# Neighbourhood attention in an encoder layer: bias tables per tile row in one transfer, split waits for queries and keys, first values on ScalarE's queue

## What is computed

```
h = rms_norm(x); proj = h @ w_in -> u, q, k, v, gates
a = fourier_mix(u) @ w_fa;  n = neighbourhood_attention(q, k, v, rpb) @ w_nb
x = x + (sig(gA) * a + sig(gB) * n) @ w_out
x = x + (silu(gate) * val) @ w_down,  [val, gate] = dwconv3(rms_norm(x) @ w_up)
return rms_norm(x)
```

## Time and profile before

| | us |
|---|---|
| median of 3 runs | 2940.61 |
| lowest and highest | 2940.39, 2942.86 |
| the profiled execution's own time | 2952.27 |
| its span, first to last instruction | 2950.5 |
| attention phase in it | about 795 to 1128 |

### The profile page before, as it was taken

One profiled execution on the slowest core, in us unless ns is written; L12 is line 12 of the kernel. 1 busy time (PEld: TensorE's weight loads), 2 busy tenths in 40 slices (PEclk: granted clock), 3 DMA queues, 4 the chain that ended last, 5 costly groups with the idle time before them and its releaser, 6 DMA issues. The chain is left out here.

```text
span 2950.5 us, 33892 instructions
## 1 busy us (share of the span) xinstructions
PE 2737.9 (93%) x12792; PEld 2274.7 (77%) x12792; DVE 1404.5 (48%) x2280; ACT 886.3 (30%) x1595; POOL 877.5 (30%) x491
## 2 busy tenths in 40 slices
PE   7999999998768896999985999997999999999997
PEld 5888888877657785777774888885888888888886
DVE  4300000006458785544336999998565554122232
ACT  3311111112345551211224444443222223343332
POOL 1010011103222224333204666664000004555553
PEclk9999999999879997999997999998999999999999
DMA  4322144426565645555535777776666665564653
GB/s 140 97 93 72 55 133 152 148 96 220 168 155 149 162 125 165 179 186 169 174 107 208 278 280 278 275 285 221 223 221 221 222 221 193 178 204 139 206 175 111
DMA packets 235537, 522.34 MB, mean 177 GB/s; under 512 B 47732, under 2 KB 73200, under 8 KB 231664
## 3 DMA queue, kind: packets, MB, share of 16 engines
q1 hardware_dynamic: 214128, 499.21, 51.3%
q10 hardware_dynamic: 21248, 20.97, 2.1%
HBM read 336.55 MB, written 185.10 MB: 177 GB/s over the span
## 5 line engine op out<-in xcount | busy, mean ns | idle before, releaser
L2205 PE MATMUL ff_psum<-ff_w,ff_hid 128*128 128x512 f32 x2112 | 479.3, 389 | 1.3 <-POOL ff_w L1798 1.3
L2205 PEld LDWEIGHTS ff_psum<-ff_w,ff_hid 128*128 128x128 f32 x2112 | 396.4, 188 | 84.1 <-POOL ff_w L1798 1.7
L1798 POOL TENSOR_TENSOR ff_w<-ff_st,ff_w 128x512 fp32r<-128x512 f32 x176 | 249.5, 1425 | 634.0 <-ACT ff_w L2041 633.6
L1798 POOL TENSOR_TENSOR ff_w<-ff_wraw,ff_w 128x512 fp32r<-128x512 f32 x154 | 269.1, 1749 | 240.9 <-ACT ff_w L2041 240.9
L422 PE MATMUL in_psum<-in_hA,in_w 128*128 128x512 f32 x1440 | 327.9, 389 | 0.0
L422 PEld LDWEIGHTS in_psum<-in_hA,in_w 128*128 128x128 f32 x1440 | 270.4, 188 | 56.0
L2166 PE MATMUL ff_psum<-ff_h,ff_w 128*128 128x512 f32 x1056 | 247.4, 393 | 27.2 <-DVE ff_h L1864 27.2
L2166 PEld LDWEIGHTS ff_psum<-ff_h,ff_w 128*128 128x128 f32 x1056 | 200.5, 190 | 70.6 <-POOL ff_w L1798 28.6
L2166 PE MATMUL ff_psum<-ff_h,ff_again 128*128 128x512 f32 x1056 | 244.7, 391 | 4.0 <-DVE ff_h L1864 4.0
L2166 PEld LDWEIGHTS ff_psum<-ff_h,ff_again 128*128 128x128 f32 x1056 | 199.3, 189 | 45.9 <-issue 4.4
L1464 PE MATMUL mo_psum<-mo_act,mo_w 128*128 128x512 f32 x768 | 191.8, 407 | 33.8 <-POOL mo_act L1315 21.0
(11 more groups left out here) (181 smaller groups left out, 4031.2 us busy)
## 6 DMA issues: line engine op xcount, KB each, us to landing
split<-ff_w SPq DMA_DIRECT2D x154, 512.0 KB, 3.6
ff_again<-split SPq DMA_DIRECT2D x154, 512.0 KB, 4.1
ff_st<-in_w_down_dram SPq DMA_DIRECT2D x176, 256.0 KB, 2.9
ff_wraw<-in_w_up_dram SPq DMA_DIRECT2D x44, 512.0 KB, 5.7
hidden<-ff_c SPq DMA_DIRECT2D x44, 512.0 KB, 3.0
ff_kraw<-hidden SPq DMA_DIRECT2D x44, 512.0 KB, 4.3
at_bias<-shifted SPq DMA_DIRECT2D x72, 256.0 KB
in_raw<-in_w_in_dram SPq DMA_DIRECT2D x32, 512.0 KB, 5.0
```

The source lines that it names most:

```text
L1798: nc.gpsimd.tensor_tensor(split_out(i, 1), parts(i), f32(split_out(i, 0)), ALU.subtract).then_inc(w_tail, 1)
L2205: last = nc.tensor.matmul(ps[:, 4 * (1 - half) + t], hid[:, a, (b * PAIRS + pair) % 2, q, t * P:(t + 1) * P], weights(i)[:, e], start=(r = ...
```

## The change

The DRAM tensor `shifted` gets the order head, query column, row, column kind, key column, and the bias and window tiles the order row kind, row, column kind, key column. So the three tables of a tile-row kind are one transfer of 768 KB, whose row for a partition is one run of 6 KB; its outermost count stays 8. In DVE's and POOL's instructions a table is now 16 rows of 32 floats, 96 floats apart. There is one bias semaphore for each row kind; SP waits, before it issues a kind's tables for head h, for that kind's tables of head h-1. `qk_in` becomes `q_in` and `k_in`: SP issues a head's queries as soon as `q_tail` of the head before is done, then waits for `k_tail` and issues the keys; ACT's first query part waits for the queries alone and its first key part for the keys. Head 0's value transfers move from SP's queue, behind three bias tables, to ACT's, ahead of its first casts.

```diff
-                sp.dma_start(shifted[j, :, c], padded[:, :, BASE_C[j] - c:BASE_C[j] - c + KC]
+                sp.dma_start(shifted[:, c, :, j], padded[:, :, BASE_C[j] - c:BASE_C[j] - c + KC]
...
-            for half in range(2):
-                for dst, src in ((qraw, qT), (kraw, kT)):
+            for dst, src, landed in ((kraw, kT, k_in), (qraw, qT, q_in)):
+                for half in range(2):
...
-                                 src[0:HEAD_DIM, :]).then_inc(qk_in, 16)
+                                 src[0:HEAD_DIM, :]).then_inc(landed, 16)
...
-        bias = m.sb("bias", [P, 2, NB, KR * KC])
-        window = m.sb("window", [P, NB, KR * KC])
+        bias = m.sb("bias", [P, 2, KINDS, KR, KINDS, KC])
+        window = m.sb("window", [P, KINDS, KR, KINDS, KC])
...
+        def load_values(engine, h):
+            run = VG * HEAD_DIM
+            for j in range(TJ):
+                rows = v[h]
+                src = bass.AP(rows.tensor, rows.offset + COL0[j] * run, [[GRID_W * run, 4], [run, KC], [1, run]])
+                engine.dma_start(vs[:, h % 2, j * VG:(j + 1) * VG].rearrange("p g d -> p (g d)"), src
+                                 ).then_inc(v_in[h % 2], 16)
...
-                for j in range(KINDS):
...
-                    rows = shifted[j, h]
-                    src = bass.AP(rows.tensor, rows.offset + (BASE_R[i] - (QR - 1)) * KC,
-                                  [[KC, QR], [REL_R * KC, QC], [1, KR * KC]])
-                    sp.dma_start(bias[:, h % 2, i * KINDS + j], src).then_inc(
-                        first_in if h == i == 0 else bias_in[h % 2], 16)
...
+                rows = shifted[h]
+                run = KINDS * KC
+                src = bass.AP(rows.tensor, rows.offset + (BASE_R[i] - (QR - 1)) * run,
+                              [[run, QR], [REL_R * run, QC], [1, KR * run]])
+                sp.dma_start(bias[:, h % 2, i].rearrange("p r j c -> p (r j c)"), src).then_inc(bias_in[i], 16)
+
+            def load_raw(h):
+                for dst, src, landed, split in ((qraw, qT, q_in, q_tail), (kraw, kT, k_in, k_tail)):
+                    sp.wait_ge(split, whole(h - 1))
+                    for half in range(2):
+                        sp.dma_start(dst[half * HEAD_DIM:(half + 1) * HEAD_DIM].rearrange("p r c -> p (r c)"),
+                                     src[h * HEAD_DIM:(h + 1) * HEAD_DIM, :]).then_inc(landed, 16)
 
             def load(h):
-                if h:
-                    sp.wait_ge(q_tail, whole(h - 1))
-                    sp.wait_ge(k_tail, whole(h - 1))
...
+                if h == 0:
+                    for i in range(KINDS):
+                        load_bias(0, i)
+                    return
+                load_raw(h)
                 if h >= 2:
                     sp.wait_ge(s_red, TILES * (h - 1))
-                if h == 0:
-                    load_bias(0, 0)
-                    load_values(0)
-                    load_bias(0, 1)
-                    load_bias(0, 2)
-                    return
                 for i in range(KINDS):
+                    sp.wait_ge(bias_in[i], 16 * h)
                     load_bias(h, i)
                 if h >= 2:
                     sp.wait_ge(o_mm, TILES * (h - 1))
-                load_values(h)
+                load_values(sp, h)
...
-                       in1=bias[:, h % 2, kind], scale=-1.0, scalar=3.0e38,
+                       in1=bias[:, h % 2, KIND[i], :, KIND[j]], scale=-1.0, scalar=3.0e38,
...
-                b = bias[:, h % 2, kind]
-                V.tensor_tensor(b, b, window[:, kind], ALU.add).then_inc(bias_ready, 1)
+                dve.wait_ge(bias_in[kind // KINDS], 16 * (h + 1))
+                b = bias[:, h % 2, KIND[i], :, KIND[j]]
+                V.tensor_tensor(b, b, window[:, KIND[i], :, KIND[j]], ALU.add).then_inc(bias_ready, 1)
...
-                if part == (0 if h else PARTS):
-                    act.wait_ge(qk_in, 64 * (h + 1))
+                if part % PARTS == 0:
+                    act.wait_ge((q_in, k_in)[part // PARTS], 32 * (h + 1))
...
+            load_values(act, 0)
             for part in (PARTS, PARTS + 1, 0, PARTS + 2, PARTS + 3, 1, 2, 3):
                 qk_head(0, part)
```

More of the change, by code:

```diff
@@ L465, in _, with fourier_phase @@
                     n += 1
-def fourier_phase(nc, step, steps, low, raw, qk_in, qT, kT, u, pos_table, chan_table, fnT_out, gate_w, b_gate, gT_out):
+def fourier_phase(nc, step, steps, low, raw, q_in, k_in, qT, kT, u, pos_table, chan_table, fnT_out, gate_w, b_gate, gT_out):
     A = SEQ // P
@@ L855, in window_mask, with attention_phase @@
     return np.concatenate([rows.reshape(P, KINDS * KR), cols.reshape(P, KINDS * KC)], axis=1)
-def attention_phase(nc, const_in, low, raw, qk_in, qT, kT, v, shifted, mask, eye, atT_out):
+def attention_phase(nc, const_in, low, raw, q_in, k_in, qT, kT, v, shifted, mask, eye, atT_out):
     KT = KR * KC // P
@@ L887, in attention_phase @@
         ps = m.banks()
-        v_in, bias_in = m.sems("v_in", 2), m.sems("bias_in", 2)
+        v_in, bias_in = m.sems("v_in", 2), m.sems("bias_in", KINDS)
         sides_in, window_done = m.sem("sides_in"), m.sem("window_done")
-        first_in = m.sem("first_in")
         qk_heads, q_tail, k_tail, bias_ready = (m.sem(x) for x in ("qk_heads", "q_tail", "k_tail", "bias_ready"))
@@ L936, in load @@
-            def load(h):
-                if h:
-                    sp.wait_ge(q_tail, whole(h - 1))
-                    sp.wait_ge(k_tail, whole(h - 1))
[L940 to L943, removed]
+                rows = shifted[h]
@@ L978, in window_kind @@
                 down = bass.AP(c.tensor, c.offset, [c.ap[0], [0, KR], [1, KC]])
-                G.tensor_tensor(window[:, i * KINDS + j].rearrange("p (r c) -> p r c", c=KC), across, down,
+                G.tensor_tensor(window[:, i, :, j], across, down,
                                 ALU.add).then_inc(window_done, 1)
@@ L1019, in reduce @@
                     dve.wait_ge(p_exp, n - 2)
-                V.tensor_tensor_reduce(out=neg[:, n % 3], in0=ps[:, SB[n % 3]],
-                                       in1=bias[:, h % 2, kind], scale=-1.0, scalar=3.0e38,
+                V.tensor_tensor_reduce(out=neg[:, n % 3].rearrange("p (r c) -> p r c", c=KC),
+                                       in0=ps[:, SB[n % 3]].rearrange("p (r c) -> p r c", c=KC),
+                                       in1=bias[:, h % 2, KIND[i], :, KIND[j]], scale=-1.0, scalar=3.0e38,
                                        op0=ALU.add, op1=ALU.min, accum_out=negmax[:, n:n + 1]).then_inc(s_red, 1)
@@ L2232, in encoder_layer @@
     padded = scratch("padded", HEADS, REL_R, REL_C)
-    shifted = scratch("shifted", KINDS, HEADS, QC, REL_R, KC)
+    shifted = scratch("shifted", HEADS, QC, REL_R, KINDS, KC)
     hidden = scratch("hidden", D_FF, SEQ)
@@ L2240, in encoder_layer @@
         step, steps = Pool(nc, outer, "in").sem("step"), [0]
-        qk_in = Pool(nc, outer, "at").sem("qk_in")
+        q_in, k_in = Pool(nc, outer, "at").sem("q_in"), Pool(nc, outer, "at").sem("k_in")
         with ExitStack() as ctx:
@@ L2246, in encoder_layer @@
                         gate_w, padded, shifted)
-            fourier_phase(nc, step, steps, low, raw, qk_in, qT, kT, u, pos_table, chan_table, fnT, gate_w, b_gate, gT)
-            attention_phase(nc, const_in, low, raw, qk_in, qT, kT, v, shifted, mask, eye, atT)
+            fourier_phase(nc, step, steps, low, raw, q_in, k_in, qT, kT, u, pos_table, chan_table, fnT, gate_w, b_gate, gT)
+            attention_phase(nc, const_in, low, raw, q_in, k_in, qT, kT, v, shifted, mask, eye, atT)
         mixer_output_phase(nc, const_in, step, steps, x, fnT, atT, gT, w_mix, w_out, norm2_g, eye, x2, hT)
```

## The result

| | us |
|---|---|
| median after (5 runs) | 2965.58 (2961.61 to 2969.40) |
| median before, same chip (5 runs) | 2942.86 (2940.39 to 2951.70) |
| ratio | 1.0074, interval 1.0054 to 1.0093 |
| profiled execution of after: own time, span | 2965.58, 2963.8 |
| forecast | 2923.6, range 2904 to 2944 |

The forecast had the wrong sign, and the time lies outside its range. Three points of the prediction came out within 2.5 us all the same: when the first values arrive, when reduce 16 comes, and what a clean head takes. They come first, because what is left after them is the cause. The timeline of after at the start of the attention: ACT issues the first values, PE waits for them, DVE's reduces 16, 32, 64, 96 and 112 (columns as in the earlier trace rows).

The account below looks back on a forecast made before the run. The attention was taken as bound by four DMA engines and compute at once. Limits of 1064 and 1067.5 us for reduce 112 gave 1072 against 1089.0: 17 us gained, 2923.6 in the median's terms, range 2904 to 2944.

Parts of the forecast that it names:

- when reduce 16 comes: DVE's reduce 16 in the attention: forecast at 877 us, where it was at 866.1.
- a clean head: An attention head without stalls, at the pace of compute: 31.75 us.
- the cost of a head on the four engines: Attention, four DMA engines carrying nearly everything: 11.8 + 10.9 + 7.5 + 3.3 = 33.5 us a head.
- Bias merged: One bias transfer with 6 KB rows: 11.8 us a head on the four engines, 12.2 if longer rows gained nothing.
- Queries ahead of keys: ACT's waits for keys in the attention go, up to 32.4 us; values slowed by 3.3 us a head.
- First values: Head 0's values on ACT's queue alternate packets with SP's rows, land at 847; the start loses 11 us.
- Strided tables, fewer issues, semaphores: Attention: strided reduces and mask additions taken at zero, at worst 70 us; issues 9 to 3 a head, hidden; semaphore waits harmless.
- A: Rival: the four engines take the attention heads over, 38.8 us a head, +7 us, 2947.6; chance 0.15.
- B: Rival: the change does less, attention heads at 36 to 37 us by the engines, 2934 to 2941; chance 0.13.

Follow-up runs that it names:

- e13: The kernel before with each value transfer cut into four of 32 partitions, on all sixteen engines: 2918.7 us, ratio 0.9922.
- e9: The changed kernel with value transfers cut in four and bias transfers in eight, over sixteen engines, first values on SP's queue: 2906.7 us, ratio 0.9872.
- e3: The kernel before with only the split of queries and keys, queries issued after their own tail: 2946.6 us, ratio 1.0029.
- e12: The changed kernel, new layout kept, each merged bias transfer cut into three with rows of 2 KB: 2945.5 us, ratio 1.0005.
- e18: The changed kernel, new layout kept, each merged bias transfer issued as two with rows of 3 KB: 2947.4 us, ratio 1.0013.
- e1: The changed kernel with head 0's values back on SP's queue, behind the first bias transfer: 2966.3 us, ratio 1.0092.
- e4: The kernel before with only the merged bias transfers and their semaphores for each row kind: 2980.0 us, ratio 1.0140.
- e6: The changed kernel with 6 KB runs described as three of 2 KB; packets stayed 6144 bytes, so a repeat of it: 2973.6 us, ratio 1.0092.
- e2: The changed kernel with the bias as nine tables of 2 KB rows in the old layout again: 2941.5 us, ratio 1.0001.
- e15: The kernel before with only head 0's values moved to ACT's queue: 2940.9 us, ratio 0.9996.
- e14: The kernel before with only one bias semaphore for each row kind, and SP's wait for it: 2938.9 us, ratio 1.0009.

## Why the prediction was wrong

**The step that failed** is the cost of a head on the four engines: 11.8 for bias, 10.9 + 3.3 for values and 7.5 for queries and keys, 33.5 us in the sum. The first two rates came from stretches in which one kind of row moves alone, and 7.5 lay between two such rates. By the records of after the three terms are 15.8, 14.6 and 9.0, 39.3 us, and the head measured 37.9. The bias term is the one most in error (4.0 us), then queries and keys (1.5); the values with their slowing were right (0.4). The records have every row's duration. Their means between reduce 16 and reduce 112, times a head's rows on one of the four engines (144, 96 or 48 of bias, 128 of values, 16 of queries and keys; in e13 32 of values, in e9 24 of bias and 32 of values), against the head as measured:

| kernel | one row: bias, values, query/key | a head's rows | a head measured |
|---|---|---|---|
| before, second profile | 0.093, 0.093, 0.547 | 13.4 + 11.9 + 8.8 = 34.1 | 34.8 |
| before, first profile | 0.101, 0.101, 0.572 | 14.5 + 12.9 + 9.2 = 36.6 | 37.1 |
| e3 | 0.106, 0.106, 0.561 | 15.2 + 13.5 + 9.0 = 37.8 | 37.7 |
| e12 | 0.106, 0.106, 0.556 | 15.3 + 13.6 + 8.9 = 37.8 | 38.2 |
| e18 | 0.148, 0.112, 0.563 | 14.2 + 14.3 + 9.0 = 37.5 | 38.2 |
| after | 0.329, 0.114, 0.561 | 15.8 + 14.6 + 9.0 = 39.3 | 37.9 |
| e1 | 0.320, 0.126, 0.578 | 15.4 + 16.1 + 9.2 = 40.8 | 39.1 |
| e4 | 0.372, 0.104, 0.589 | 17.9 + 13.3 + 9.4 = 40.6 | 41.6 |
| e6 | 0.358, 0.117, 0.568 | 17.2 + 14.9 + 9.1 = 41.2 | 38.9 |
| e2 | 0.105, 0.105, 0.556 | 15.2 + 13.5 + 8.9 = 37.5 | 36.6 |
| e13 | 0.108, 0.108, 0.544 | 15.6 + 3.5 + 8.7 = 27.7 | 32.5 |
| e9 | 0.523, 0.136, 0.530 | 12.6 + 4.4 + 8.5 = 25.4 | 32.7 |

(In the kernels of nine tables, bias and value rows are both 2 KB and share a mean.) Where four engines carry the values, the sum gives the head within 1.7 us in nine of ten profiles and within 2.3 in e6. Where sixteen do, it is 4.8 and 7.3 us below the head, and the head is near the 31.75 of compute. Another view of the records agrees: from reduce 16 to reduce 112 at least four rows are on their way for 95% of the time in both profiles of before and 96% in after, but for 86% in e13. The rows of bias that took 0.085 us alone took up to 0.106 in the mean over the heads, so the sum tells that the engines are busy, not what they could do at best. So the kernel before already ran at the pace of the four engines: a wait for keys that is taken away leaves the rows where they are, and comes back for queries. The sum of undisturbed rates, 32.6 in the prediction, was 1.5 to 4 us a head short of the sums for before, 9 to 24 over six, as much as the gain of 17 us that was forecast.

**Bias merged.** Forecast 11.8 us a head, measured 15.8 in after and 17.9 in e4, against 13.4 to 14.5 in before. I carried over the rate of 8 KB rows from 789:793, and these are a store (`fnT` from `ft_u`, issued at 789.09), not a load, and took no gain (12.2 us) as the bad end; a loss by the merge stood in no case. The Trainium skill (DMA: Bandwidth & Descriptors, "Why a DMA increments its semaphore by 16 and not by 1") says that the outermost counts decide how many engines a transfer uses, and that part is borne out: e13 changes nothing but the outermost count of the value transfers, by cutting them, and the time falls by 0.8%. In these sums the merge is worth 1.3 to 4.5 us of a head; e4's start is 12 us later than in the second profile of before.

It is shown that the merge into few transfers with long rows does it, and neither the layout nor the order (e12, e18 against after and e1). Why a 6 KB row takes 0.234 us at one time and 0.455 at another, with eight engines at work in both, is open. The rows of neighbouring engines start 384 bytes apart in DRAM and overlap, and in e4 they get faster while the transfers go on (median 0.466 us at 924, 0.345 at 936, 0.234 at 944), which would suit engines that read the same place at first and drift apart. But in after they stay near 0.455 from 880 to 896, and pieces of 2 and 3 KB overlap too. The cause may as well lie where the rows are written, as each of the eight engines fills 16 partitions of its own; the slow rows take about twice the time of the quick ones, as do those of queries and keys. No run varies the destination alone. All this is argued only.

**Queries ahead of keys.** The cost (values slowed while queries load) was named, at 3.3 us a head; by e3 the head is 2.9 us longer than in the second profile of before and 0.6 longer than in the first. The gain was the error: 32.4 us of stalls, taken from one profile, where another has 18. With 194.8 us for six heads e13, which keeps the order, takes back 14 to 28 us of them; so they were the engines' time, not the order's. In e3 the start did gain, 7 us.

**First values.** Right in its mechanism, one row of ACT's queue after one of SP's: 847 forecast, 849.2 measured; 877 and 877.4. One term inside was off and did not bind: queries were put at 822 to 825, and ACT had them at 835.0. But the landing was counted as a loss of 11 us on the path, and e1 shows it as none. While the values wait, the engines move what is needed later, and the next heads have it sooner; a start gained is kept only if computation, not transfers, sets the heads' pace. e15 can't tell, as its start is no later than that of before (863.4). The Trainium skill (DMA: Bandwidth & Descriptors, "Issuing engines are not separate DMA queues") says that transfers from different issuing engines run on the same DMA engines and interleave, and that a second one saves issue time alone. The total agrees (e15, 0.9996), while in after the first values came 33 us later.

**Strided tables, fewer issues, semaphores.** Right: masks and reduces take 0.69, and e12 and e14 cost nothing that can be told from none.

**The rivals.** A had the mechanism, and the 37.7 us a head from which it decides was passed (37.9). Its 38.8 came from other terms than those that came true, slow queries in place of long bias rows, and its time, 2947.6, was 18 us short, as no case had the merge as a loss. It had 0.15. B's condition (36 to 37 us a head by the engines) was the state of before itself in the first profile; its upper time, 2941, does not follow from its 1086, which gives 2937.6.

## What to carry to other kernels

When a few DMA engines carry most rows, add up the mean durations of all their rows over the whole loop, other traffic included, and compare the sum with the loop's period before reading any wait. Where they agreed here, order and semaphores won nothing (e3, e14), and cutting a transfer so that more engines share it won 0.8% with one edit (e13). Merging small transfers changes the length of the row; treat its rate as unknown in both directions until a row of that length, from that source to that destination, has been seen. Take a second profile before turning a sum of stalls into a forecast.

## What the hardware showed that was not expected

- Loads with rows of 6 KB from overlapping places ran at 119 GB/s on eight engines for 16 us, and at 207 later; kernels with rows of 2 and 3 KB in the same layout could not be told from before (1.0005, 1.0013).
- Sixteen engines moved 430 and 412 GB/s in loads of other phases, but 197 to 228 in those of the attention, where eight moved 204 to 207 and four 101 to 103. With sixteen at work a row of 8 KB took 0.309 us in the one case and 0.627 in the other, and a row of 4 KB half of it, so length was not what mattered.
- Two queues on the same engines passed packets one for one though one queue's were larger (158 and 128 packets, 1.04 and 0.25 MB): the first values, 128 rows of 2 KB on each engine, landed 33 us later beside rows of 6 and 8 KB.
- SP was held for 21.8 us over the issue of four value transfers, so the queries behind them were issued 5.5 us after what they wait for was done.
